# Layer 0's feed-forward in a two-layer fp32 backbone: both halves of the context's columns as one moving operand of 512, their partial sums added on VectorE

## The chip, the cores and the metric

The kernel runs on one core of one Trainium2 chip. The metric is the device time of one execution in microseconds (us), lower is better. All sums below are made on one profiled execution of the kernel before.

## What is computed

A two-layer backbone over 512 latent tokens and 256 context tokens, width 1024, everything in fp32. Each layer has an attention sub-layer and a channel sub-layer. The change touches the channel sub-layer of layer 0 alone. Cut to what matters (latents and context run through the same weights, each with its own shift, scale and gate):

```python
def conv_ffn(h, w_up, conv_w, conv_b, w_down):
    u = h @ w_up                                   # 1024 -> 2 * 2816
    u = depthwise_conv_width_3(u, conv_w) + conv_b # along the tokens
    g, v = jnp.split(u, 2, axis=-1)
    return (jax.nn.silu(g) * v) @ w_down

hx = modulate(rmsnorm(x_lat, g_ffn[l]), sh2x, sc2x)
x_lat = x_lat + g2x * conv_ffn(hx, w_up[l], conv_w[l], conv_b[l], w_down[l])
if not last:                                       # layer 0 only
    hc = modulate(rmsnorm(x_ctx, g_ffn[l]), sh2c, sc2c)
    x_ctx = x_ctx + g2c * conv_ffn(hc, w_up[l], conv_w[l], conv_b[l], w_down[l])
```

The last layer has no context in its feed-forward, so a context product of the feed-forward exists in layer 0 only.

## The kernel before

**Products in three parts.** Activations lie with their features on the partitions and the 768 tokens along the free dimension: latents in columns 0 to 511, context in 512 to 767. Each fp32 factor is split into a high half (rounded to the fp32r type) and a low half (the rest): weights `w_hi` and `w_lo`, activations `h_hi` and `h_lo` (input of the up-projection), `a_hi` and `a_lo` (input of the down-projection). For each block k of 128 input features the function `three` issues three matmuls into one PSUM bank: w_hi with the high half, w_hi with the low half, w_lo with the high half (lines 1289, 1290, 1291). Each has its own weight load.

**Units.** A unit is 128 output features. It has two PSUM banks: bank `bank_of(c)` for the 512 latent columns, the next for the 256 context columns (`groups` is `[(0, 512), (512, 768)]` in layer 0). Four units take turns in the eight banks (`RING` = 4), and four slots in `w_hi` and `w_lo` do so too. The up-projection has 44 units in layer 0 (22 pairs of a g unit and a v unit), each over 8 blocks k. They come in three parts of 8, 8 and 6 pairs (`PARTS`); behind each part come 8 down units over as many k as the part had pairs, so 22 k for each of the 8 output tiles.

**TensorE's order in layer 0's feed-forward.** `first_units` does the first three up units together, k by k, latents first, since each k of `h_hi`, `h_lo` comes just then from VectorE. Then `feature_unit` does one unit after the other: all k of the latents, then all k of the context. `down_start` does the first two down units of a part in two batches: all but the last two k, then these, behind a wait for the last pair's `a_lo` (`a_lo_done`). The last four down units of the last part are `tail_units`: the latents of all four, then the context of all four, with the sums of squares (L1255) and the spreading of the norm's factor (L1235) between. Then layer 1's projection begins, `first_tiles`, again k by k as VectorE delivers `h_lo`.

**What follows a unit.** For an up unit ScalarE (L2112) writes the convolution's middle tap and bias from PSUM to `conv_g` or `conv_v`, one instruction for the latents and one for the context. Then it rounds the next weights of this slot (`unit_hi`, L1737, from `w_raw`), GpSimd subtracts them for `w_lo` (L1164), and that frees the `w_raw` buffer for a DMA from the queue on SyncE. VectorE (L2666) adds the two outer taps from PSUM, latents and context each, with one wait on itself between the two taps. For a pair it then multiplies (L2675), ScalarE rounds (`a_hi`, L2121), VectorE subtracts (`a_lo`, L2678). Between pairs VectorE also reduces tiles of the modulation's weights (`ada_tile`, L2158). For a down unit VectorE adds the gated result into `x_sb` (`update`, L2621, in the tail `update_part`, L2333), latents and context each one instruction.

**The tail on VectorE.** `tail` mixes, in a fixed order: updates of the four last tiles (L2333), sums of squares (L2261, fed by ScalarE's squares), the reciprocal for the norm (L2255), one weight split (L2208), and for each k the next layer's normed input (`ht`, L2288, and `h_lo`, L2296). The context's updates of tiles 2 and 3 stand between the latents' k, the context's norm factor behind the last of them:

```python
for k in range(1, KT):
    part_scaled(j, 0, k)
    part_lo(j, 0, k - 1)
    if k in (1, 3):
        update_part(1, 2 + k // 2)
    if k in (2, 4):
        add_part(j, 1, 1 + k // 2)
part_lo(j, 0, KT - 1)
part_scales(j, 1)
```

## Time and profile before

| | us |
|---|---|
| median of 3 runs | 1715.58 |
| lowest and highest of them | 1715.50, 1716.35 |
| span of the profiled execution, its own time | 1715.9 |
| TensorE busy in it | 1643.9 |
| VectorE busy in it | 1101.3 |
| ScalarE busy in it | 773.7 |
| GpSimd busy in it | 634.2 |

The profiled execution has no time of its own beside the span from its first to its last instruction. Layer 0's feed-forward lies between 456.7 us (first matmul of its up-projection) and 1010.5 us (first matmul of layer 1) of that span. PE is TensorE's matmul, PEld its weight load, DVE VectorE, ACT ScalarE, POOL GpSimd. Matmuls overlap: the duration in a row is longer than the distance from one start to the next, and the distance is what a matmul costs in a row of them.

### The profile page before, as it was taken

The numbers are of one execution on the slowest core, as the hardware profiler recorded it, in microseconds if no ns is written. First come the engines' busy times: TensorE is split into PE (matmuls) and PEld (weight loads), VectorE is DVE, ScalarE is ACT, GpSimd is POOL, SyncE is SP. The second block draws the span as 40 slices with busy tenths as digits, with TensorE's granted clock in tenths as the row PEclk, the third lists the DMA queues.
The fourth block names the chain that finished last, engine by engine and source line by source line (L and its number), as shares of the span: only waits on it lengthen the run. The fifth ranks groups of instructions, "written<-read, shape, count | busy, mean of one in ns | idle before, by whom it ended". The sixth has DMA issues, their size and how long they took to land.

```text
span 1715.9 us, 25956 instructions
## 1 busy us (share of the span) xinstructions
PE 1643.9 (96%) x9530; PEld 1393.6 (81%) x9530; DVE 1101.3 (64%) x1728; ACT 773.7 (45%) x1281; POOL 634.2 (37%) x328
## 2 busy tenths in 40 slices
PE   5899999989999999999999999999989999999998
PEld 3778887768898888888888877788767888888887
DVE  7887678878965575676245774777665763353256
ACT  6546666553443312332133344676564543343343
POOL 0356562220132243333332307664322244444442
PEclk9899999999999999999999999999999999999999
DMA  9430000024223243444434422101112133223332
GB/s 394 176 109 26 26 26 26 26 98 185 80 97 106 98 135 100 133 125 132 136 111 134 147 98 87 38 14 38 38 34 103 62 112 99 97 98 98 95 93 95
DMA packets 44509, 168.24 MB, mean 98 GB/s; under 512 B 4736, under 2 KB 4736, under 8 KB 42496
## 3 DMA queue, kind: packets, MB, share of 16 engines
q1 hardware_dynamic: 41760, 158.08, 27.7%
q10 hardware_dynamic: 2656, 8.91, 1.4%
q8 instruction: 60, 0.98, 0.2%
q14 instruction: 33, 0.27, 0.1%
HBM read 161.73 MB, written 5.24 MB: 97 GB/s over the span
## 4 chain that ended last, share of the span: by engine, by line
PE 70%; DVE 6%; issue 3%; ACT 2%; POOL 1%; DMA 1%; DVEq 0%; ACTq 0%; POOLq 0%
PE ps L1289 21%; PE ps L1290 21%; PE ps L1291 21%; PE ps L1420 3%; PE ps L1434 2%; DVE sqsum L2261 1%; PE ps L1453 1%; POOL w_lo L1164 1%; DVE ht L2288 1%; PE ps L1454 1%; DVE junk_mid L2191 1%; DMA w_raw<-w_d 1%; DVE h_lo L2296 1%; ACT p_sb L1966 0%; ACT w_hi L1737 0%
## 5 line engine op out<-in xcount | busy, mean ns | idle before, releaser
L1164 POOL TENSOR_TENSOR w_lo<-w_raw,w_hi 128x1024 fp32r<-128x1024 f32 x175 | 441.3, 2524 | 915.4 <-ACT w_hi L1737 882.7
L1289 PE MATMUL ps<-h_hi,w_hi 128*128 128x512 f32 (+1 forms) x1592 | 567.7, 357 | 10.8 <-DVE h_lo L2296 6.5
L1290 PE MATMUL ps<-h_lo,w_hi 128*128 128x512 f32 (+1 forms) x1592 | 556.1, 349 | 0.0
L1291 PE MATMUL ps<-h_hi,w_lo 128*128 128x512 f32 (+1 forms) x1592 | 555.4, 349 | 0.0
L1289 PEld LDWEIGHTS ps<-h_hi,w_hi 128*128 128x128 f32 x1592 | 302.5, 190 | 59.3 <-issue 21.0
L1291 PEld LDWEIGHTS ps<-h_hi,w_lo 128*128 128x128 f32 x1592 | 302.3, 190 | 39.7
L1290 PEld LDWEIGHTS ps<-h_lo,w_hi 128*128 128x128 f32 x1592 | 302.9, 190 | 35.3
L1737 ACT ACTIVATE w_hi<-w_raw 128x1024 fp32r<-128x1024 f32 x188 | 198.4, 1056 | 227.9 <-PE ps L1291 209.8
L1289 PE MATMUL ps<-a_hi,w_hi 128*128 128x512 f32 (+1 forms) x552 | 191.6, 347 | 1.2 <-DVE a_lo L2678 1.2
L1290 PE MATMUL ps<-a_lo,w_hi 128*128 128x512 f32 (+1 forms) x552 | 191.3, 347 | 0.0
L1291 PE MATMUL ps<-a_hi,w_lo 128*128 128x512 f32 (+1 forms) x552 | 191.0, 346 | 0.0
L2666 DVE SCALAR_TENSOR_TENSOR conv_v<-ps,sm,conv_v 128x511 f32<-128x511 f32 (+1 forms) x132 | 83.2, 658 | 140.3 <-ACT conv_v L2112 134.0
L2463 DVE TENSOR_REDUCE nb<-ps 128x1 f32<-128x768 f32 (+1 forms) x160 | 128.8, 843 | 11.2 <-PE ps L1420 10.9
L1211 POOL TENSOR_TENSOR p_sb<-p_sb,ri 128x768 f32<-128x768 f32 (+1 forms) x80 | 105.2, 1335 | 77.5 <-DVE ri L2470 77.5
L2488 DVE TENSOR_TENSOR pt_lo<-ps,pt_hi 128x512 fp32r<-128x512 f32 (+1 forms) x160 | 105.9, 673 | 40.0 <-ACT pt_hi L1976 39.4
L2666 DVE SCALAR_TENSOR_TENSOR conv_g<-ps,sm,conv_g 128x511 f32<-128x511 f32 (+1 forms) x132 | 83.1, 658 | 69.1 <-ACT conv_g L2112 57.5
L1966 ACT ACTIVATE p_sb<-ps,nb 128x768 f32<-128x768 f32 (+1 forms) x120 | 97.1, 813 | 62.0 <-DVE nb L2463 51.6
L2621 DVE SCALAR_TENSOR_TENSOR x_sb<-ps,mod,x_sb 128x512 f32<-128x512 f32 x72 | 45.3, 657 | 121.9 <-PE ps L1291 121.6
L2112 ACT ACTIVATE conv_v<-ps,sm 128x512 f32<-128x512 f32 x66 | 44.3, 705 | 166.8 <-PE ps L1291 166.8
L1976 ACT ACTIVATE pt_hi<-ps 128x512 fp32r<-128x512 f32 (+1 forms) x160 | 91.5, 586 | 59.6 <-PE ps L1434 56.0
L2158 DVE CUSTOM_DVE_ANT_0 ada_junk<-ada_b,c_bc 128x1024 bf16<-128x1024 f32 x80 | 117.0, 1463 | 2.0 <-DMA ada_b<-ada_d 0.7
L1289 PEld LDWEIGHTS ps<-a_hi,w_hi 128*128 128x128 f32 x552 | 104.5, 189 | 14.7 <-DVE a_lo L2678 1.6
(189 smaller groups left out, 2410.7 us busy)
## 6 DMA issues: line engine op xcount, KB each, us to landing
w_raw<-w_d SPq DMA_DIRECT2D x188, 512.0 KB, 3.5
ada_b<-ada_d SPq DMA_DIRECT2D x56, 512.0 KB, 4.3
ada_first<-first_d SPq DMA_DIRECT2D x8, 1024.0 KB, 20.3
ada_lead<-ada_d SPq DMA_DIRECT2D x14, 512.0 KB, 3.9
ada_mid<-ada_d SPq DMA_DIRECT2D x10, 512.0 KB, 7.8
x_sb<-x_d SPq DMA_DIRECT2D x2, 1536.0 KB, 8.8
x_sb<-x_d ACTq DMA_DIRECT2D x1, 3072.0 KB, 11.6
x_spill_d<-x_sb ACTq DMA_DIRECT2D x1, 2048.0 KB, 7.5
```

The costliest lines, as they stand in the source:

```text
L1164: nc.gpsimd.tensor_tensor(w_lo[:, c % RING, :], w_raw[:, c % RAW, :], w_hi[:, c % RING, :].bitcast(f32), ALU.subtract).then_inc(w_lo_done, 1)
L1211: nc.gpsimd.tensor_tensor(buf, buf, ri[:, r:r + 1].broadcast_to([P, k]), ALU.mult).then_inc(scaled_done, 1)
L1289: nc.tensor.matmul(out, lh, rh, start=first, stop=False)
L1290: nc.tensor.matmul(out, lh, rl_, start=False, stop=False)
L1291: return nc.tensor.matmul(out, ll, rh, start=False, stop=last)
L1737: A(w_hi[:, c % RING, :], w_raw[:, c % RAW, :], ACT.Copy).then_inc(w_hi_done, 1)
L1966: A(dst, src, ACT.Exp, bias=nb[:, sid % 8:sid % 8 + 1], accum_out=total).then_inc(exp_done, 1)
L1976: A(pt_hi[tid % TURNS][:, 0:n], ps[:, 4 + tid % TURNS, 0:n], ACT.Copy).then_inc(pt_hi_done, 1)
L2158: ins = V.tensor_tensor_reduce(junk[:, :], buf[:, :], silu_c[:, s, :], 1.0, 0.0, ALU.mult, ALU.add, dst(s))
L2463: V.tensor_reduce(nb[:, sid % 8:sid % 8 + 1], src, AX.X, ALU.max, negate=True).then_inc(bias_done, 1)
L2488: V.tensor_tensor(lo[:, 0:n], ps[:, 4 + tid % TURNS, 0:n], hi[:, 0:n].bitcast(f32), ALU.subtract) \
L2666: ins = V.scalar_tensor_tensor(dst, src, sm[:, bass.ds(8 * i + w, 1)], dst, ALU.mult, ALU.add)
```

## The change

In layer 0's feed-forward the context's product of a block k is made by two matmuls in place of three. `h_hi` and `h_lo` become the two planes of one tensor `h_both`, `a_hi` and `a_lo` those of `a_both` (the same addresses as before for `h`, and for `a`). One matmul takes w_hi with a moving operand of 2 x 256 columns, the high half's context columns and the low half's, and writes 512 columns of the context's bank. The second takes w_lo with the high half and adds to the first 256 of them. The bank then holds two partial sums of 256 columns, and VectorE adds them: for an up unit by a reduction over two strided elements into `ctx_sum` in SBUF, after which it also makes the context's middle tap and bias itself (ScalarE does the latents' only), and the outer taps of the context read `ctx_sum`; for a down unit by one more gated add into `x_sb`. In the tail the second add waits for the first. The latents, layer 1, the attention's products and the output projection stay as they are.

```diff
+            def beside(c, lhs, both, k, first, last):
+
+                lh, ll = lhs
+                out = ps[:, bank_of(c) + 1, :]
+                both = both[:, :, k, SEQ:TOK]
+
+                def low():
+                    return nc.tensor.matmul(out[:, 0:CTX], ll, both[:, 0, :], start=False, stop=False)
+
+                if not first:
+                    low()
+                mm = nc.tensor.matmul(out[:, 0:2 * CTX].rearrange("p (a t) -> p a t", a=2), lh, both, start=first, stop=last)
+                return low() if first else mm
...
                 for g, (t0, t1) in enumerate(groups):
                     for k in range(kn):
                         col = slice(k * P, (k + 1) * P)
-                        mm = three(ps[:, bank_of(c) + g, 0:t1 - t0], (w_hi[:, c % RING, col], w_lo[:, c % RING, col]),
-                                   (mh[:, k, t0:t1], ml[:, k, t0:t1]), k == 0, k == kn - 1)
+                        lhs = w_hi[:, c % RING, col], w_lo[:, c % RING, col]
+                        if g == 1:
+                            mm = beside(c, lhs, moving, k, k == 0, k == kn - 1)
+                        else:
+                            mm = three(ps[:, bank_of(c), 0:t1 - t0], lhs,
+                                       (moving[:, 0, k, t0:t1], moving[:, 1, k, t0:t1]), k == 0, k == kn - 1)
...
-                                for g, (t0, t1) in enumerate(groups):
-                                    ins = A(buf[:, t0:t1], tile_out(l, c, g), ACT.Identity,
-                                            bias=sm[:, bass.ds(8 * i + (wcol + 3), 1)],
-                                            scale=sm[:, bass.ds(8 * i + (wcol + 1), 1)])
-                                ins.then_inc(conv_started, 1)
+                                A(buf[:, 0:SEQ], tile_out(l, c, 0), ACT.Identity,
+                                  bias=sm[:, bass.ds(8 * i + (wcol + 3), 1)],
+                                  scale=sm[:, bass.ds(8 * i + (wcol + 1), 1)]).then_inc(conv_started, 1)
                                 unit_hi(c + RING, i)
...
+                    sums = [ps[:, bank_of(c + n) + i, 0:t1 - t0]]
+                    if j % 2 == 0 and in_halves(l, g):
+                        sums = half_sums(c + n)
+                    for m, src in enumerate(sums):
+                        ins = V.scalar_tensor_tensor(xs, src, mod[:, g, l * N_ADA + gate + d:l * N_ADA + gate + d + 1],
+                                                     xs, ALU.mult, ALU.add)
+                        if m < len(sums) - 1:
+                            step(ins)
+                    ins.then_inc(bank_read if i else tail_read, 1)
...
+                    if halves:
+                        step.mark(add(1, half_sums(c)[0]))
+                    ins = add(0, ps[:, bank_of(c), 0:SEQ])
+                    if halves:
+                        step.wait()
+                        ins = add(1, half_sums(c)[1])
+                    elif len(groups) > 1:
+                        ins = add(1, ps[:, bank_of(c) + 1, 0:CTX])
                     ins.then_inc(bank_read, 1)
...
+                                if l == 0:
+                                    wait_tile(dve, c, i)
+                                    two = ps[:, bank_of(c) + 1, 0:2 * CTX].rearrange("p (a t) -> p t a", a=2)
+                                    step(V.tensor_reduce(ctx_sum[:, gv, :], two, AX.X, ALU.add))
+                                    step.mark(V.tensor_scalar(buf[:, SEQ:TOK], ctx_sum[:, gv, :],
+                                                              sm[:, bass.ds(8 * i + (wcol + 1), 1)],
+                                                              sm[:, bass.ds(8 * i + (wcol + 3), 1)], ALU.mult, ALU.add))
                                 dve.wait_ge(conv_started, 4 * i + (2 * (pair0 + half) + gv + 1))
-
+                                if l == 0:
+                                    step.wait()
                                 for tap in range(2):
                                     w = wcol + 2 * tap
                                     for g, (t0, t1) in enumerate(groups):
                                         dst = buf[:, t0 + 1:t1] if tap == 0 else buf[:, t0:t1 - 1]
                                         n_ = t1 - t0
-                                        whole = tile_out(l, c, g)
+                                        whole = ctx_sum[:, gv, :] if g == 1 else tile_out(l, c, g)
```

`first_units`, `down_start` and `tail_units` call `beside` for the context in the same way. `step(ins)` is an instruction and a wait of VectorE for its end; `step.mark` counts it, `step.wait` waits later.

## Rows read from the trace of the kernel before

**Rows 1.** The page, busy time of the span and the chain that ended last.
```profile
PE 1643.9 (96%) x9530; PEld 1393.6 (81%) x9530; DVE 1101.3 (64%) x1728; ACT 773.7 (45%) x1281; POOL 634.2 (37%) x328
...
PE 70%; DVE 6%; issue 3%; ACT 2%; POOL 1%; DMA 1%; DVEq 0%; ACTq 0%; POOLq 0%
```
**Rows 2.** Windows: stretch, its length, busy of each engine (instructions), granted clock.
```profile
456.70:999.80 543.10, 543.04 (x3105) 479.63 (x3106) 334.43 (x495) 170.44 (x228) 173.32 (x64) 1.00 0.36 118
```
**Rows 3.** Groups by line and form, PE, window 456.7:999.8: count, busy, mean ns.
```profile
L1289 PE MATMUL ps<-h_hi,w_hi 128*128 128x256 f32 x352 | 99.4, 282 | 0.0
...
L1291 PE MATMUL ps<-a_hi,w_lo 128*128 128x256 f32 x152 | 43.0, 283 | 0.0
```
**Rows 4.** Timeline, PE, two runs of one form: start, duration (us).
```profile
480.07 0.28 PE L1290 MATMUL ps<-h_lo,w_hi 128*128 128x256 f32 x1
...
482.71 0.28 PE L1291 MATMUL ps<-h_hi,w_lo 128*128 128x256 f32 x1
482.83 0.40 PE L1289 MATMUL ps<-h_hi,w_hi 128*128 128x512 f32 x1
...
484.21 0.39 PE L1289 MATMUL ps<-h_hi,w_hi 128*128 128x512 f32 x1
...
488.07 0.39 PE L1291 MATMUL ps<-h_hi,w_lo 128*128 128x512 f32 x1
```
**Rows 5.** Timeline, PE, layer 0's first tiles: three of 512, three of 256, again.
```profile
53.56 0.40 PE L1289 MATMUL ps<-h_hi,w_hi 128*128 128x512 f32 x1
...
54.61 0.40 PE L1289 MATMUL ps<-h_hi,w_hi 128*128 128x512 f32 x1
```
**Rows 6.** Groups by line and form, DVE and, last, ACT, whole span.
```profile
L2463 DVE TENSOR_REDUCE nb<-ps 128x1 f32<-128x768 f32 x128 | 116.5, 950 | 10.4 <-PE ps L1420 10.1
...
L2463 DVE TENSOR_REDUCE nb<-ps 128x1 f32<-128x256 f32 x32 | 12.3, 416 | 0.8 <-PE ps L1420 0.8
...
L2621 DVE SCALAR_TENSOR_TENSOR x_sb<-ps,mod,x_sb 128x256 f32<-128x256 f32 x24 | 11.4, 475 | 0.0
...
L2479 DVE TENSOR_SCALAR rl<-ri,nlam,first_sum 128x1 f32<-128x1 f32 x40 | 10.9, 273 | 1.4
...
L2112 ACT ACTIVATE conv_v<-ps,sm 128x512 f32<-128x512 f32 x44 | 34.3, 779 | 166.8 <-PE ps L1291 166.8
```
**Rows 7.** Timeline, DVE and ACT, one pair of part 1 and the first taps.
```profile
726.44 2.42 DVE L2666 SCALAR_TENSOR_TENSOR conv_v<-ps,sm,conv_v 128x511 f32<-128x511 f32 x4 [4.46 <-ACT conv_v L2112]
...
731.70 0.96 DVE L2678 TENSOR_TENSOR a_lo<-conv_g,a_hi 128x768 f32 x1 [1.16 <-ACT a_hi L2121]
...
725.06 1.24 ACT L2112 ACTIVATE conv_v<-ps,sm 128x512 f32<-128x512 f32 x2 [6.08 <-PE ps L1291]
...
485.32 1.14 DVE L2666 SCALAR_TENSOR_TENSOR conv_g<-ps,sm,conv_g 128x511 f32<-128x511 f32 x2 [0.16 <-DVE conv_g L2666]
```
**Rows 8.** Timeline, the end of part 2's up-projection: DVE, then PE.
```profile
965.28 0.96 DVE L2678 TENSOR_TENSOR a_lo<-conv_g,a_hi 128x768 f32 x1 [1.16 <-ACT a_hi L2121]
...
966.64 0.40 PE L1289 MATMUL ps<-a_hi,w_hi 128*128 128x512 f32 x1
```
**Rows 9.** Timeline, the tail and layer 1's start: DVE, then PE.
```profile
995.83 0.75 DVE L2333 SCALAR_TENSOR_TENSOR x_sb<-ps,mod,x_sb 128x512 f32<-128x512 f32 x1 [2.73 <-PE ps L1291]
...
1003.61 0.18 DVE L2255 RECIPROCAL n_r<-n_sd 128x4 f32<-128x4 f32 x1 [1.06 <-ACT n_sd L1747]
...
1006.62 1.23 DVE L2208 TENSOR_TENSOR w_lo<-w_raw,w_hi 128x1024 fp32r<-128x1024 f32 x1 [0.34 <-ACT w_hi L1737]
...
1012.71 0.43 DVE L2261 TENSOR_TENSOR sqsum<-sqsum,sqt 128x256 f32<-128x256 f32 x1 [0.83 <-ACT sqt L1871]
...
1014.37 0.48 DVE L2333 SCALAR_TENSOR_TENSOR x_sb<-ps,mod,x_sb 128x256 f32<-128x256 f32 x1
...
1014.51 0.50 PE L1289 MATMUL ps<-h_hi,w_hi 128*128 128x512 f32 x1 [0.93 <-DVE h_lo L2296]
...
1021.73 0.71 PE L1235 MATMUL ps<-sm,n_r 128*128 128x128 f32 x4 [1.71 <-DVE n_r L2255]
```

More of the change, by code:

```diff
@@ L707, in backbone @@
     sqsum = place("sqsum", [P, TOK], f32, R_QKV + 48 * KB)
-    h_hi = place("h_hi", [P, KT, TOK], f32r, R_H)
-    h_lo = place("h_lo", [P, KT, TOK], f32r, R_H + 24 * KB)
+    h_both = place("h_both", [P, 2, KT, TOK], f32r, R_H)
+    h_hi, h_lo = h_both[:, 0, :, :], h_both[:, 1, :, :]
     y_sb = place("y_sb", [P, 2, KT, SEQ // 2], f32, R_H)
@@ L713, in backbone @@
     ol = place("ol", [P, KT, TOK], f32r, R_QKV + 24 * KB)
-    a_hi = place("a_hi", [P, 8, TOK], f32r, R_QKV)
-    a_lo = place("a_lo", [P, 8, TOK], f32r, R_QKV + 24 * KB)
+    a_both = place("a_both", [P, 2, 8, TOK], f32r, R_QKV)
+    a_hi, a_lo = a_both[:, 0, :, :], a_both[:, 1, :, :]
     o_sb = place("o_sb", [P, KT, TOK], f32, R_O)
@@ L718, in backbone @@
     conv_v = place("conv_v", [P, TOK], f32, R_O + 3 * KB)
+    ctx_sum = place("ctx_sum", [P, 2, CTX], f32, R_O + 22 * KB)
     sqt = place("sqt", [P, 2, TOK], f32, R_O)
@@ L1016, in tile_out, with in_halves, half_sums @@
             return ps[:, bank_of(c) + g, 0:t1 - t0]
+        def in_halves(l, g):
+            return l == 0 and g == 1
+        def half_sums(c):
+            return ps[:, bank_of(c) + 1, 0:CTX], ps[:, bank_of(c) + 1, CTX:2 * CTX]
         stat_order = [("norm", 0, 0)]
@@ L1275, in tail_units @@
                                 lhs = (w_hi[:, w[0], w[1]], w_lo[:, w[0], w[1]])
-                                rhs = (moving[0][:, k, t0:t1], moving[1][:, k, t0:t1])
+                                rhs = (moving[:, 0, k, t0:t1], moving[:, 1, k, t0:t1])
                             else:
                                 lhs, rhs = half_weights(l, KT - TAIL + n, k, True), half_output(k, True, t0, t1)
-                            mm = three(ps[:, bank_of(c + n) + i, 0:t1 - t0], lhs, rhs, k == 0, k == kn - 1)
+                            if moving and in_halves(l, g):
+                                mm = beside(c + n, lhs, moving, k, k == 0, k == kn - 1)
+                            else:
+                                mm = three(ps[:, bank_of(c + n) + i, 0:t1 - t0], lhs, rhs, k == 0, k == kn - 1)
                         mm.then_inc(unit_done if i else tail_done, 1)
@@ L1597, in feature_unit @@
                     pe.wait_ge(bank_read, 4 * i + (evac_index(c) - 3))
-                mh, ml = moving
                 for g, (t0, t1) in enumerate(groups):
@@ L1618, in first_units @@
                             w = ((c + j) % RING, slice(k * P, (k + 1) * P))
-                            mm = three(part_out(norm, c + j, i),
-                                       (w_hi[:, w[0], w[1]], w_lo[:, w[0], w[1]]),
-                                       (h_hi[:, k, t0:t1], h_lo[:, k, t0:t1]), k == 0, k == KT - 1)
+                            lhs = w_hi[:, w[0], w[1]], w_lo[:, w[0], w[1]]
+                            if g == 1:
+                                mm = beside(c + j, lhs, h_both, k, k == 0, k == KT - 1)
+                            else:
+                                mm = three(part_out(norm, c + j, i), lhs, (h_hi[:, k, t0:t1], h_lo[:, k, t0:t1]),
+                                           k == 0, k == KT - 1)
                             if k == KT - 1 and i == 1:
@@ L1679, in down_start @@
                                 w = ((c + j) % RING, slice(k * P, (k + 1) * P))
-                                mm = three(ps[:, bank_of(c + j) + g, 0:t1 - t0],
-                                           (w_hi[:, w[0], w[1]], w_lo[:, w[0], w[1]]),
-                                           (a_hi[:, k, t0:t1], a_lo[:, k, t0:t1]), k == 0, k == n - 1)
+                                lhs = w_hi[:, w[0], w[1]], w_lo[:, w[0], w[1]]
+                                if g == 1:
+                                    mm = beside(c + j, lhs, a_both, k, k == 0, k == n - 1)
+                                else:
+                                    mm = three(ps[:, bank_of(c + j), 0:t1 - t0], lhs,
+                                               (a_hi[:, k, t0:t1], a_lo[:, k, t0:t1]), k == 0, k == n - 1)
                         if ks[0] > 0:
@@ L2614, in _, with update, add @@
                     ada_late(2)
-                def update(c, gate, x_col):
+                def update(c, gate, x_col, halves=False):
                     wait_tile(dve, c)
-                    for g, (t0, t1) in enumerate(groups):
-                        xs = x_sb[:, x_col, t0:t1]
-                        ins = V.scalar_tensor_tensor(xs, ps[:, bank_of(c) + g, 0:t1 - t0],
-                                                     mod[:, g, l * N_ADA + gate + x_col:l * N_ADA + gate + x_col + 1],
-                                                     xs, ALU.mult, ALU.add)
+                    def add(g, src):
+                        xs = x_sb[:, x_col, groups[g][0]:groups[g][1]]
+                        factor = mod[:, g, l * N_ADA + gate + x_col:l * N_ADA + gate + x_col + 1]
+                        return V.scalar_tensor_tensor(xs, src, factor, xs, ALU.mult, ALU.add)
+                    if halves:
[6 more added lines that the diff above has]
+                        ins = add(1, ps[:, bank_of(c) + 1, 0:CTX])
                     ins.then_inc(bank_read, 1)
@@ L2697, in _ @@
                     if l == 0:
-                        per += [4, 5, 1][part]
+                        per += [4, 5, 1][part] + 2 * 2 * 2
                     split = l == DEPTH - 1 and part == 0
@@ L2707, in _ @@
                         c = down_unit(l, part) + d
-                        update(c, 5 * KT, d)
+                        update(c, 5 * KT, d, in_halves(l, len(groups) - 1))
                         if l == 0 and d < ADA_IN_DOWN[part]:
```

12 lines of the change are left out of this document (5 added, 7 removed).

## The prediction

> **What bounds the kernel now.** I read the page first. TensorE is busy for 96% of the span and carries 70% of the chain that ended last, VectorE 6% of it [rows 1]. So the question for every part of the change is whether it lies on TensorE's path. The stretch that the change touches, by its window, is tighter still: from 456.7 to 999.8 us TensorE is busy for 543.04 of 543.10 us at the full granted clock (1.00, that is 2.4 GHz), VectorE for 334, ScalarE for 170 [rows 2]. The reader is to see that there is no wait there to be removed: a gain can only come from fewer nanoseconds in TensorE's own row of matmuls, and VectorE has 209 us of room. The tail behind it is another matter: there TensorE waits for VectorE twice, 0.93 and 1.71 us [rows 9].
>
> Next the timeline, for what one matmul costs in a row of them. 22 distances of the form 256 take 2.64 us (480.07 to 482.71), 120.0 ns each; 17 of the form 512 take 3.86 us (484.21 to 488.07), 227.1 ns each [rows 4]. The second 256 columns cost 107.1 ns, so the first 256 cost the same plus 12.9 ns. That 12.9 ns is the fixed share of a matmul with its weight load, and it is what the change can save.
>
> **The change part by part: TensorE.** Three matmuls of 256 columns (360.0 ns) become one of 512 and one of 256 (347.1 ns). The columns streamed are the same 768, the weight loads go from three to two: 12.9 ns less for each k. The forms' counts say how often: 352 such k in the up-projections and 152 in the down-projections of this stretch, 504 in all [rows 3]; 24 more lie in the tail.
>
> The row of matmuls now changes its form at almost every step. What such changes cost is to be seen in layer 0's first tiles, where three of 512 and three of 256 take turns: one round takes 1.05 us (53.56 to 54.61) against 3 x 347.1 = 1.041 us, 9 ns more for one change each way [rows 5]. With runs of one, the bounds are nothing and the whole 9 ns for each k. I take 3 ns, a third, since the excess could be spread over the three matmuls that follow the change as well as sit on the first. That leaves 10 ns for each k: 504 x 0.010 = 5.0 us, with ends of 504 x 0.004 = 2.0 and 504 x 0.0129 = 6.5 us.
>
> The moving operand now lies in two pieces of 256 columns. No row shows such an operand. The bounds: nothing, or, if the second piece begins like a matmul of its own, 2 x 120.0 - 227.1 = 13 ns for each k, which would take the whole saving. I see no reason for a gain from it, and take nothing, as an address step is nearer to the middle of a matmul than to a new one.
>
> The Trainium skill ("TensorE: Matmul & The Clock Gate", Back-to-back issue gap) gives N / 2.4 + 2.5 ns from one matmul to the next at full clock. By it the three matmuls cost 327.5 ns and the two 325.0, and the change would be worth 504 x 0.0025 = 1.3 us. The trace disagrees: its fixed share is 12.9 ns [rows 4].
>
> **VectorE and ScalarE in the up units.** ScalarE loses its context instruction: of 1.24 us for both [rows 7] 0.78 stay [rows 6]. VectorE gets a reduction over 512 PSUM elements; rows for 256 and 768 elements take 416 and 950 ns, so 0.68 us between them. It is strided, which no row shows; its end could lie up to twice as high. Then a wait for itself, 0.16 us as between the taps [rows 7], then the context's middle tap over 256 elements of SBUF. For that there is only a form of one element, 0.27 us, and a two-tensor form of 256, 0.48 [rows 6]; I take 0.40. Then 0.16 again. The taps could start 0.68 + 0.16 + 0.40 + 0.16 = 1.40 us behind the unit's end. Before, they started 726.44 - 725.06 = 1.38 us behind it, as they waited for ScalarE [rows 7]. So nothing is late for a unit whose end VectorE waits for. The Trainium skill ("VectorE: DVE Perf Modes", The TRN2 errata) has 58 + 256/2 cycles, 0.19 us, for the tap if it runs in the doubled mode. No row here shows that mode; it would make the start earlier by 0.2 us, with the same sum.
>
> VectorE's work grows by about 2 x 1.4 = 2.8 us for a pair. In a pair of part 1 it stands idle 4.46 + 1.16 = 5.6 us of the 16.7 that TensorE takes [rows 7], so it still fits. Behind VectorE's added wait stand only its own taps, and behind these the PSUM bank and ScalarE. The bank is wanted four units later: the first taps end at 486.5 us [rows 7] and TensorE wants that bank when the unit started at 482.83 [rows 4] has ended, 24 x (0.227 + 0.120) = 8.3 us on, at 491.2. A delay of 1.4 us is covered by 4.7. `w_hi`, `w_lo` and the DMA behind them come a little sooner, since ScalarE rounds after a shorter instruction; TensorE waits for none of them here, so this is worth nothing.
>
> The tightest place is the end of part 2's up-projection. The last `a_lo` ends at 966.24 us and TensorE wants it at 966.64, 0.40 us later [rows 8]. TensorE comes 8 x 0.010 = 0.08 us sooner, the pair's chain starts 0.02 later: 0.3 us of cover stay. If the added instructions took 1 us more than I sum, that would cost 0.7 us, once.
>
> **VectorE in the down units.** One more instruction of 0.48 us [rows 6] for each of 20 units outside the tail, with the wait placed behind the latents' add, so hardly a stall. TensorE's unit takes 6 to 8 us beside it. Four of them lie before the tail, about 1.8 us that VectorE brings with it; it is waiting 2.73 us for TensorE before the third tail update [rows 9], which takes them up.
>
> **The tail.** Here VectorE is the path, and the two adds of a tile depend on each other: 0.48 + 0.16 = 0.64 us more for each of four tiles. Tile 0's lies under the wait of 1.06 us for the norm's root. Tile 1's meets 0.34 us of idle before the weight split [rows 9] and a context that ends 0.07 us sooner: 0.23 late. Tile 2's makes that 0.87, of which the 0.83 us of idle before its squares (ScalarE, itself behind a weight's DMA) take all but 0.04. Tile 3's, at 1014.37, meets no idle. So the norm factor, for which TensorE waits 1.71 us at 1021.73 [rows 9], comes 0.68 us later, and layer 1 with it. The 24 k saved in the tail end in those waits and are worth nothing. Bounds: 0 if the waits absorb all, 2.6 if all four are exposed.
>
> **Sum.** 1715.9 - 5.0 + 0.7 = 1711.6 us on the profiled execution's scale. It lies 0.3 us above the median of the runs, so the forecast for the median is 1711.3, call it 1711.2. A difference of 0.2%, 3.4 us, is about what a measurement of this kernel can tell from none; the edges are 1712.1 and 1719.0.
>
> **The rivals.**
>
> A. The forecast: 9 to 13 ns saved for each k, a small loss in the tail. 1709 to 1712. For it: 256 more columns cost 107.1 ns, which is 2.4 GHz to half a nanosecond, so the rest of either form is no streaming, and TensorE never waits in the stretch. Chance 0.62.
>
> B. Too little is saved to be seen. If the full 9 ns of a change each way falls on each k, 4 ns stay: 2.0 - 0.7 = 1.3 us, 1714.3. The same outcome follows if the fixed share belongs to something that two matmuls of unlike form do not share. By the Trainium skill's gap ("TensorE: Matmul & The Clock Gate", Back-to-back issue gap) it would be 1.3 - 0.7, 1715.0, the same case. For it: the round of six really is longer [rows 5]. Against it: in that round the change touches one matmul in three. Chance 0.25, all of it within 0.2%.
>
> C. The split operand costs a fixed share of its own: 347.1 + 13 + 3 ns against 360.0 for each k, 1.5 us lost, and 0.7 in the tail: 1717.8. It decides against the change from 9 ns on, and visibly from 17 ns on. Chance 0.08, half of it above 1719.0.
>
> D. VectorE becomes what TensorE waits for in the loop of pairs: a wait for `bank_read` or `w_lo` takes the place of free running. Its price: from 5.6 us of added work for a pair on, each further microsecond is paid in each of 22 pairs; at 6.6 us it is 22 - 4.3 = 18 us, 1733. That needs the strided reduction at some 2.6 us in place of 0.68. Against it: VectorE has 209 us of room [rows 2]. Chance 0.05, slower.
>
> **The numbers.** Faster 0.62, same 0.25 + 0.04 = 0.29, slower 0.09. The range goes from 1709.0 (12.9 ns saved in full, the tail almost free) to 1716.8 (beyond B, into the milder half of C).
>
> **What would show it.** After the change, the distances in TensorE's row within the context's k should sum to about 350 ns for one 512 and one 256; 347 means that changes of form are free, 356 is rival B, 363 rival C. VectorE's busy time in the stretch should rise by some 60 us, ScalarE's fall by 20, and TensorE's idle time should stay under 1 us. In the tail the wait for `n_r` should grow by 0.7 us. I am wrong if a wait for `bank_read`, `w_lo` or `a_lo` appears inside the stretch, or if the pair of matmuls leaves 345 to 353 ns.

## The result, and the profile after

The changed kernel takes 1746.95 us (median of 4 runs, 1742.62 to 1749.37) against 1715.96 of the kernel before (4 runs beside it, 1715.50 to 1720.17). The ratio is 1.017, with a 95% interval of 1.015 to 1.019: 31 us slower, where I forecast 4 us faster and put the upper end of my range at 1716.8. The profiled execution has a span of 1745.3 us, against 1715.9.

First the page of the changed kernel, the busy times and the chain that ended last.

```profile
PE 1645.8 (94%) x9002; PEld 1367.9 (78%) x9002; DVE 1224.2 (70%) x1840; ACT 755.3 (43%) x1237; POOL 625.0 (36%) x328
...
PE 52%; DVE 17%; issue 9%; ACT 3%; DVEq 1%; POOL 1%; DMA 0%; ACTq 0%; SPq 0%; POOLq 0%
```

TensorE has its 528 fewer matmuls (9530 in [rows 1], 9002 now), but VectorE's busy time grew by 123 us and its share of the chain from 6% to 17%. Next, what TensorE waited for from the first up unit to the tail's end: us in total, times, longest.

```profile
PE ps L1315 <- DVE a_both L2734: 24.4, 3, 11.2
PE ps L1315 <- DVE h_both L2329: 2.3, 2, 1.8
PE ps L1244 <- DVE n_r L2288: 1.7, 1, 1.7
PE ps L1315 <- DVE conv_g L2722: 1.4, 2, 0.8
```

L2734 is the subtraction that was `a_lo`. It makes TensorE wait three times, once at the end of each part: 24.4 us in a stretch that had no wait at all [rows 2]. L2722 are the outer taps, which free a PSUM bank: 1.4 us. Both are waits that the prediction named as signs of its being wrong. `n_r` is the wait of [rows 9], unchanged at 1.7.

Then the windows of the changed kernel: stretch, length, busy us of PE, PEld, DVE, ACT and POOL (instructions), granted clock, DMA share, GB/s.

```profile
457.00:998.00 541.00, 515.23 (x2460) 431.47 (x2459) 430.07 (x570) 142.16 (x172) 154.25 (x61) 0.97 0.34 111
...
613.00:619.00 6.00, 5.52 (x14) 4.42 (x15) 4.67 (x12) 1.06 (x1) 0.14 (x1) 0.52 0.27 87
```

VectorE is busy for 430 us where it was for 334 [rows 2], and TensorE for 515 of 541. Behind the first wait the granted clock is 0.52. The timeline of TensorE there:

```profile
603.35 0.40 PE L1309 MATMUL ps<-a_both,w_hi 128*128 128x512 f32 x1
613.48 0.80 PE L1315 MATMUL ps<-a_both,w_hi 128*128 128x512 f32 x1 [9.73 <-DVE a_both L2734]
614.07 0.63 PE L1316 MATMUL ps<-a_both,w_hi 128*128 128x512 f32 x1
614.50 0.63 PE L1317 MATMUL ps<-a_both,w_lo 128*128 128x512 f32 x1
...
618.77 0.41 PE L1315 MATMUL ps<-a_both,w_hi 128*128 128x512 f32 x1
619.01 0.40 PE L1316 MATMUL ps<-a_both,w_hi 128*128 128x512 f32 x1
```

After standing for 9.7 us TensorE comes back at 1.2 GHz: 0.43 us from one matmul of 512 to the next, until 618.77, then 0.24 us. Those 5.29 us hold 11 matmuls of 512 and 2 of 256, which at the distances of [rows 4] are 2.74 us; so the wait costs some 2.6 us more than its own length. The second wait (11.2 us, up to 826.00) is followed by 4.4 us at half clock, worth 2.1. After the third (3.5 us, up to 993.12) TensorE runs 1.0 us at full clock and then 3.3 us at 0.51, worth 1.6. That is 6.3 us in all. From the first up matmul to the tail's first sums of squares the trace has 574.2 us, before 545.4: 28.9 us more. The parts give 24.4 + 1.4 + 6.3, less the 4.2 that TensorE saved (measured in e2_tensor_only below): 27.9. The last 1.0 us is not accounted for.

### The profile page after: what moved, and what is told of

Read it like the earlier page. It is cut to its first block, busy times and chain, and to the rows that moved or that the text cites. A ratio compares the mean times of both kernels' runs of the same rounds, so it can differ in the third digit from the quotient of the medians.

```text
span 1745.3 us, 25175 instructions
## 1 busy us (share of the span) xinstructions
PE 1645.8 (94%) x9002; PEld 1367.9 (78%) x9002; DVE 1224.2 (70%) x1840; ACT 755.3 (43%) x1237; POOL 625.0 (36%) x328
## 4 chain that ended last, share of the span: by engine, by line
PE 52%; DVE 17%; issue 9%; ACT 3%; DVEq 1%; POOL 1%; DMA 0%; ACTq 0%; SPq 0%; POOLq 0%
PE ps L1315 14%; PE ps L1317 13%; PE ps L1316 13%; PE ps L1446 3%; PE ps L1309 3%; DVE conv_g L2722 2%; PE ps L1460 2%; DVE conv_v L2722 2%; DVE ctx_sum L2708 1%; PE ps L1305 1%; DVE ada_junk L2191 1%; DVE conv_g L2731 1%; DVE conv_g L2709 1%; ACT a_both L2154 1%; DVE mod L2748 1%
## 5 line engine op out<-in xcount | busy, mean ns | idle before, releaser
L1315 PE MATMUL ps<-h_both,w_hi 128*128 128x512 f32 (+1 forms) x1240 | 468.0, 377 | 12.7 <-DVE h_both L2329 7.9
L1317 PE MATMUL ps<-h_both,w_lo 128*128 128x512 f32 (+1 forms) x1240 | 456.0, 368 | 0.0
L1316 PE MATMUL ps<-h_both,w_hi 128*128 128x512 f32 (+1 forms) x1240 | 455.7, 367 | 0.0
L1315 PEld LDWEIGHTS ps<-h_both,w_hi 128*128 128x128 f32 x1240 | 234.7, 189 | 59.9 <-issue 23.0
L1317 PEld LDWEIGHTS ps<-h_both,w_lo 128*128 128x128 f32 x1240 | 234.6, 189 | 39.6
L1316 PEld LDWEIGHTS ps<-h_both,w_hi 128*128 128x128 f32 x1240 | 235.2, 190 | 35.5
L1315 PE MATMUL ps<-a_both,w_hi 128*128 128x512 f32 (+1 forms) x376 | 143.9, 383 | 26.5 <-DVE a_both L2734 25.7
L2191 DVE CUSTOM_DVE_ANT_0 ada_junk<-ada_b,c_bc 128x1024 bf16<-128x1024 f32 x80 | 145.5, 1819 | 1.3
L1317 PE MATMUL ps<-a_both,w_lo 128*128 128x512 f32 (+1 forms) x376 | 143.0, 380 | 0.0
L1316 PE MATMUL ps<-a_both,w_hi 128*128 128x512 f32 (+1 forms) x376 | 142.9, 380 | 0.0
L1309 PE MATMUL ps<-h_both,w_hi 128*128 128x512 f32 x352 | 127.5, 397 | 0.0
L2662 DVE SCALAR_TENSOR_TENSOR x_sb<-ps,mod,x_sb 128x512 f32<-128x512 f32 (+1 forms) x92 | 53.1, 616 | 101.6 <-PE ps L1317 67.1
L2722 DVE SCALAR_TENSOR_TENSOR conv_v<-ps,sm,conv_v 128x511 f32<-128x511 f32 x88 | 66.0, 750 | 58.7 <-ACT conv_v L2146 49.3
L1315 PEld LDWEIGHTS ps<-a_both,w_hi 128*128 128x128 f32 x376 | 72.0, 191 | 40.3 <-DVE a_both L2734 27.0
```

Source lines behind the costliest of these rows:

```text
L1309: mm = nc.tensor.matmul(out[:, 0:2 * CTX].rearrange("p (a t) -> p a t", a=2), lh, both, start=first, stop=last)
L1315: nc.tensor.matmul(out, lh, rh, start=first, stop=False)
L1316: nc.tensor.matmul(out, lh, rl_, start=False, stop=False)
L1317: return nc.tensor.matmul(out, ll, rh, start=False, stop=last)
L2191: ins = V.tensor_tensor_reduce(junk[:, :], buf[:, :], silu_c[:, s, :], 1.0, 0.0, ALU.mult, ALU.add, dst(s))
L2722: ins = V.scalar_tensor_tensor(dst, src, sm[:, bass.ds(8 * i + w, 1)], dst, ALU.mult, ALU.add)
```

## Why VectorE is late: the same instruction at two prices

VectorE's groups by form in the stretch of the feed-forward of the changed kernel: busy us, mean ns of one, then idle time before.

```profile
L2191 DVE CUSTOM_DVE_ANT_0 ada_junk<-ada_b,c_bc 128x1024 bf16<-128x1024 f32 x80 | 145.5, 1819 | 1.3
L2722 DVE SCALAR_TENSOR_TENSOR conv_g<-ctx_sum,sm,conv_g 128x255 f32<-128x255 f32 x44 | 38.6, 878 | 0.0
L2722 DVE SCALAR_TENSOR_TENSOR conv_v<-ps,sm,conv_v 128x511 f32<-128x511 f32 x44 | 33.0, 750 | 6.4
L2708 DVE TENSOR_REDUCE ctx_sum<-ps 128x256 f32<-128x512 f32 x44 | 30.2, 685 | 20.3 <-PE ps L1309 16.6 <-DVE mod L2748 1.7 <-DVE mod L2750 1.2
L2722 DVE SCALAR_TENSOR_TENSOR conv_v<-ctx_sum,sm,conv_v 128x255 f32<-128x255 f32 x44 | 27.1, 615 | 0.0
...
L2709 DVE TENSOR_SCALAR conv_g<-ctx_sum,sm 128x256 f32<-128x256 f32 x22 | 21.0, 955 | 5.1 <-DVE ctx_sum L2708 5.1
...
L2748 DVE COPY mod<-ada_sum 128x2 f32 x16 | 18.7, 1166 | 2.3
...
L2709 DVE TENSOR_SCALAR conv_v<-ctx_sum,sm 128x256 f32<-128x256 f32 x22 | 14.1, 641 | 4.2 <-DVE ctx_sum L2708 4.2
```

The reduction costs what I gave it, 0.68. But the context's outer tap, 255 elements, takes 878 ns in its mean for a g unit, longer than the latents' of 511 elements at 750, and 615 for a v unit; the middle tap takes 955 and 641 ns. Single instructions show why. VectorE, then GpSimd, at the end of part 0:

```profile
600.18 0.68 DVE L2708 TENSOR_REDUCE ctx_sum<-ps 128x256 f32<-128x512 f32 x1
601.06 1.61 DVE L2709 TENSOR_SCALAR conv_g<-ctx_sum,sm 128x256 f32<-128x256 f32 x1 [0.19 <-DVE ctx_sum L2708]
602.82 0.75 DVE L2722 SCALAR_TENSOR_TENSOR conv_g<-ps,sm,conv_g 128x511 f32<-128x511 f32 x1 [0.15 <-DVE conv_g L2709]
603.49 1.69 DVE L2722 SCALAR_TENSOR_TENSOR conv_g<-ctx_sum,sm,conv_g 128x255 f32<-128x255 f32 x1
605.33 0.75 DVE L2722 SCALAR_TENSOR_TENSOR conv_g<-ps,sm,conv_g 128x511 f32<-128x511 f32 x1 [0.15 <-DVE conv_g L2722]
606.00 0.48 DVE L2722 SCALAR_TENSOR_TENSOR conv_g<-ctx_sum,sm,conv_g 128x255 f32<-128x255 f32 x1
606.39 0.69 DVE L2708 TENSOR_REDUCE ctx_sum<-ps 128x256 f32<-128x512 f32 x1
607.27 0.41 DVE L2709 TENSOR_SCALAR conv_v<-ctx_sum,sm 128x256 f32<-128x256 f32 x1 [0.19 <-DVE ctx_sum L2708]
...
612.47 0.96 DVE L2734 TENSOR_TENSOR a_both<-conv_g,a_both 128x768 f32 x1 [1.16 <-ACT a_both L2154]
```
```profile
599.83 5.06 POOL L1173 TENSOR_TENSOR w_lo<-w_raw,w_hi 128x1024 fp32r<-128x1024 f32 x2 [13.46 <-ACT w_hi L1772]
```

GpSimd does two splits of a weight from 599.83 to 604.89, so one ends near 602.3 and the next near 604.9. The middle tap takes 0.41 us at 607.27, when GpSimd is idle, and 1.61 us at 601.06: it ends at 602.67, which is about the first split's end and its own 0.41. The outer tap takes 0.48 at 606.00 and 1.69 at 603.49: it ends at 605.18, some 0.3 us behind the second split's end (the trace is rough for GpSimd). The taps between them that read PSUM take 0.75 us, split or no split. These rows suggest that an instruction of VectorE that reads two operands from SBUF, or a TENSOR_SCALAR or COPY from SBUF to SBUF, stands still until GpSimd's running split is over, and that one with an operand in PSUM does not; e5 and e6 below test it. The change moved four outer context taps for a pair from the second kind to the first and added two middle taps of the first.

The Trainium skill ("SBUF — State Buffer", SBUF: two separate sides) states the rule: an instruction of VectorE in a two-port mode, or with two SBUF inputs where GpSimd's instruction reads SBUF too, and one of GpSimd exclude each other for the whole instruction, and the loser stands. The trace agrees, with 0.41 against 1.61 us for the middle tap and 0.48 against 1.69 for the outer one.

The sign was in the trace before. Four groups of VectorE by form, kernel before, same stretch:

```profile
L2158 DVE CUSTOM_DVE_ANT_0 ada_junk<-ada_b,c_bc 128x1024 bf16<-128x1024 f32 x80 | 117.0, 1463 | 2.0 <-DMA ada_b<-ada_d 0.7
L2675 DVE TENSOR_TENSOR conv_g<-conv_g,conv_v 128x768 f32<-128x768 f32 x22 | 34.8, 1582 | 0.8
...
L2678 DVE TENSOR_TENSOR a_lo<-conv_g,a_hi 128x768 f32 x22 | 21.1, 959 | 25.1 <-ACT a_hi L2121 25.1
...
L2692 DVE COPY mod<-ada_sum 128x2 f32 x16 | 10.8, 674 | 2.2
```

The product L2675 and the subtraction L2678 are two instructions of one form, 1582 and 959 ns: the product fell under GpSimd's split, the subtraction never did. I read only the second price.

The busy times now nearly add up. The times without a split are 413 ns for the middle tap, 475 for the outer tap, 1224 for an ada tile, 959 for the product and 178 for a copy (ada tile and copy from e5_small_split below). Against them the changed kernel stands 47.6 us in its 80 ada tiles, 23.9 in its outer taps, 16.9 in its middle taps, 15.8 in 16 copies and 3.9 in three others, 108 us; the kernel before stood 19.1 + 13.7 + 7.9 = 41 us in ada tiles, products and copies. That is 67 us more of standing, beside 58 us of real new work (44 x 0.685 + 44 x 0.413 + 20 x 0.477) and 2 us in the tail: 127, against the page's difference of 123, in which what overlaps counts once.

What it means for the pairs: in part 0 the subtraction L2734 starts at 510.15 and six pairs later at 612.47, 17.05 us for a pair, 15.6 and 18.5 in turn. TensorE takes 16 x (3 x 0.227 + 0.353) = 16.55. So VectorE does not catch up with the three units that it gets at once at the start of part 0. Part 1 has no such start, but three ada tiles for each pair in place of two, and from 694.73 to 824.98 a pair takes 18.6 us: the backlog of some 14 us grows there from the pace alone, and this part ends in the longest wait. In part 2 a pair takes 17.06 us (906.82 to 992.11), and the wait is 3.5 us.

## The experiments

**TensorE alone, VectorE alone.** Is TensorE's part worth what I summed, and is the loss all VectorE's? e2_tensor_only keeps the new matmuls and gives ScalarE and VectorE their old work (the reduction and the second adds go, and the second partial sum stays unread); e3_vector_only keeps the new ScalarE and VectorE work on the three old matmuls and adds the one partial sum to itself.

```diff
 e2_tensor_only
-        A(buf[:, 0:SEQ], tile_out(l, c, 0), ...)
+        for g, (t0, t1) in enumerate(groups): ins = A(buf[:, t0:t1], tile_out(l, c, g), ...)
...
-        whole = ctx_sum[:, gv, :] if g == 1 else tile_out(l, c, g)
+        whole = tile_out(l, c, g)
 e3_vector_only
+        return three(out[:, 0:CTX], lhs, (both[:, 0, :], both[:, 1, :]), first, last)
...
-        two = ps[:, bank_of(c) + 1, 0:2 * CTX].rearrange("p (a t) -> p t a", a=2)
+        two = ps[:, bank_of(c) + 1, 0:CTX].rearrange("p (t a) -> p t a", a=1).broadcast_to([P, CTX, 2])
```

> TensorE's part of the change alone; VectorE and ScalarE work as before and read only the first partial sum (the second, w_hi with the low half, is left out of the context's result). Theory VectorE (the loss comes from VectorE's added work alone): no wait for a_lo or a bank in layer 0's feed-forward, the clock stays at 1.00 there, and 504 pairs of matmuls at 354 ns in place of 360 give about 3 us: 1713 us. Theory TensorE (the new matmuls themselves cost): waits or longer distances stay, over 1725 us.

> The work of VectorE and ScalarE of the changed kernel alone: TensorE issues the three matmuls as before, and VectorE adds the first 256 columns to themselves in the place of the two partial sums (the context's result is about doubled before the gate). Theory VectorE: the waits at the ends of the three parts are there in full, about 11, 11 and 3.5 us, a little less since TensorE is slower: 1745 us. Theory TensorE: about 1717 us.

e2_tensor_only: 1714.91 us, ratio 0.9983 (0.9972 to 0.9993). Its stretch up to the tail takes 541.2 us against 545.4, 4.2 less, with no wait for `a_both` or a bank. e3_vector_only: 1744.79 us, ratio 1.016 (1.014 to 1.019), and TensorE's waits in it:

```profile
PE ps L1309 <- DVE a_both L2728: 21.1, 3, 10.4
...
PE ps L1309 <- DVE conv_g L2716: 0.6, 1, 0.6
```

So the loss is VectorE's side alone, and TensorE's side is a gain of some 4 us. Its timeline, e2_tensor_only, context matmuls:

```profile
490.62 0.40 PE L1309 MATMUL ps<-h_both,w_hi 128*128 128x512 f32 x1
490.85 0.28 PE L1305 MATMUL ps<-h_both,w_lo 128*128 128x256 f32 x1
490.97 0.40 PE L1309 MATMUL ps<-h_both,w_hi 128*128 128x512 f32 x1
...
492.74 0.40 PE L1309 MATMUL ps<-h_both,w_hi 128*128 128x512 f32 x1
```

Six k take 2.12 us, 353 ns for each. Three matmuls of 256 took 360.0 and two of unchanged distance would take 347.1: inside a unit the saving is 7 ns for each k, and a change of form each way costs about 6. Over the whole context of a unit, whose first k has its two matmuls in the other order, the same trace has 2.81 us for 8 k (490.16 to 492.97), 351 ns each; 504 x 8.7 ns are 4.4 us, which is the stretch's 4.2.

**The operand in two pieces.** e4_one_piece is e2_tensor_only with the moving operand of 512 taken as one piece (the latents' high half, so the context's product is another one).

```diff
+    whole, both = both[:, 0, k, 0:SEQ], both[:, :, k, SEQ:TOK]
...
-    mm = nc.tensor.matmul(out[:, 0:2 * CTX].rearrange("p (a t) -> p a t", a=2), lh, both, start=first, stop=last)
+    mm = nc.tensor.matmul(out[:, 0:2 * CTX], lh, whole, start=first, stop=last)
```

> As the run with TensorE's part alone, but the matmul of 512 reads the latents' high half, one contiguous piece, in place of the context's two pieces (the context's result is not computed). If the split operand costs, the distance behind the 512 falls from 236 to 227 to 233 ns; if the change of form costs, it stays at 233 to 236 ns.

1710.80 us in a single run, span 1709.0, stretch 541.2 us like e2_tensor_only's, and the same distances. The split operand costs nothing; rival C is out. The 4 us by which this single time lies under e2's median are not in the stretch, and I read nothing from them.

**GpSimd's split made small.** If VectorE stands for GpSimd, an eighth of the split (the rest of `w_lo` is left stale) must bring VectorE's instructions back to their prices, with all of the change kept.

```diff
-    nc.gpsimd.tensor_tensor(w_lo[:, c % RING, :], w_raw[:, c % RAW, :], w_hi[:, c % RING, :]..., ALU.subtract)
+    w = slice(0, UNIT // 8 if up_unit(0, 0) + RING <= c < unit0(1) else UNIT)
+    nc.gpsimd.tensor_tensor(w_lo[:, c % RING, w], w_raw[:, c % RAW, w], w_hi[:, c % RING, w]..., ALU.subtract)
```

> The changed kernel, but in layer 0's feed-forward GpSimd writes only the first 128 of 1024 columns of w_lo (most of the weights' low halves are stale). Theory port (VectorE's added instructions on two SBUF operands, or in the form that reads SBUF doubly, stand still while GpSimd works): their means fall from 878, 615, 955 and 641 ns to about 0.47, 0.47, 0.41 and 0.41 us, the copies to mod to 0.25, a pair takes VectorE under 15 us, TensorE waits nowhere, about 1712 us. Theory sum (the added instructions and their waits are too long in themselves): a pair still takes 16 to 18 us and the time stays over 1735.

1715.06 us, ratio 0.9984 (0.9973 to 0.9994), and no wait for `a_both`. VectorE's groups by form in it:

```profile
L2192 DVE CUSTOM_DVE_ANT_0 ada_junk<-ada_b,c_bc 128x1024 bf16<-128x1024 f32 x80 | 97.9, 1224 | 1.7 <-DMA ada_b<-ada_d 0.3
...
L2723 DVE SCALAR_TENSOR_TENSOR conv_g<-ctx_sum,sm,conv_g 128x255 f32<-128x255 f32 x44 | 21.4, 486 | 0.0
L2710 DVE TENSOR_SCALAR conv_g<-ctx_sum,sm 128x256 f32<-128x256 f32 x22 | 9.6, 436 | 5.1 <-DVE ctx_sum L2709 5.1
L2710 DVE TENSOR_SCALAR conv_v<-ctx_sum,sm 128x256 f32<-128x256 f32 x22 | 9.1, 413 | 4.2 <-DVE ctx_sum L2709 4.2
```

955 became 436 ns, 878 became 486, 1819 became 1224. Where VectorE runs through its backlog in part 0 a pair takes 13.2 and 14.5 us in turn, 13.9 in the mean. By my sum it was 16.7 - 5.6 + 2.8 = 13.9, and that agreement is luck. The pair that I summed was one of part 1 [rows 7], with three ada tiles and no copies, where part 0 has two tiles, and copies in every other pair; it held 0.7 us of a standing product; and my 5.6 us counted the 1.16 us for ScalarE's rounding as room, which e5's pairs contain. The added work itself was summed about right. A pair of part 1 without copies takes 16.7 - 4.46 - 0.68 = 11.6 us before (without its wait for the unit and the standing) and 16.63 - 1.91 = 14.7 in e5, 3.1 us more where I had 2.8. With the copies the next pair takes 16.15, so 15.4 in the mean. To TensorE's 16.55 that leaves 2.7 us of room in part 0 and 1.1 in part 1, and the changed kernel takes 3.2 us more than e5 in both, 17.05 and 18.6.

**Which form stands.** e6_taps_from_psum keeps every instruction and wait of the change, but both the middle tap and the outer taps of the context read the first partial sum in PSUM in place of `ctx_sum` (so the second partial sum is left out). e10_middle_from_psum does it for the middle tap alone, e11_outer_from_psum for the outer taps alone.

```diff
 e6, e10
-    step.mark(V.tensor_scalar(buf[:, SEQ:TOK], ctx_sum[:, gv, :], ...))
+    step.mark(V.tensor_scalar(buf[:, SEQ:TOK], half_sums(c)[0], ...))
 e6, e11
-    whole = ctx_sum[:, gv, :] if g == 1 else tile_out(l, c, g)
+    whole = half_sums(c)[0] if g == 1 else tile_out(l, c, g)
```

> The changed kernel with every instruction and wait of it, but the context's middle tap and outer taps on VectorE read the first partial sum in PSUM in place of the sum in SBUF (the second partial sum is left out of the up-projection's context). Theory port: an instruction with one SBUF operand at most does not stand still behind GpSimd, so the taps of 255 stay at 0.48 us and the middle tap at 0.4 to 0.5; a pair takes VectorE under 15.5 us and TensorE no longer waits for a_lo: 1712 to 1716 us. Theory sum: 1740 us or more.

> The changed kernel, only the context's middle tap on VectorE reads the first partial sum in PSUM; the outer taps still read the sum in SBUF (part of the context's convolution is left wrong). It takes the doubled form away and leaves the two-operand form. In the changed kernel's trace the middle tap stood still for (955 + 641 - 2 x 413) x 22 ns = 17 us, the outer taps for (878 + 615 - 2 x 475) x 44 ns = 24 us. If both forms hold VectorE, about half of the 28 us of loss stays: 1725 to 1735 us. If only the doubled form does, 1714.

> The counterpart: the outer taps of the context read PSUM, the middle tap reads the sum in SBUF in its doubled form. If both forms hold VectorE, 1718 to 1730 us, a little less than the run before, since its share was 24 of 41 us. If only the two-operand form does, 1714; if only the doubled form does, 1745.

A single run each: 1713.96, 1738.79 and 1724.78 us. TensorE's wait for `a_both` is 24.4 us in the changed kernel, and in e6, e10 and e11 in this order:

```profile
PE ps L1315 <- DVE a_both L2734: 1.5, 2, 0.9
```
```profile
PE ps L1315 <- DVE a_both L2734: 18.8, 3, 8.9
```
```profile
PE ps L1315 <- DVE a_both L2734: 8.0, 2, 5.1
```

Both forms hold VectorE, the outer taps' two SBUF operands more (22 us of time come back without them, 8 without the middle tap's, 33 without both). The time that one form loses is partly taken over by the next that meets the split. In e11 the middle tap stands longer than in the changed kernel (955 ns there):

```profile
L2709 DVE TENSOR_SCALAR conv_g<-ctx_sum,sm 128x256 f32<-128x256 f32 x22 | 25.0, 1134 | 5.1 <-DVE ctx_sum L2708 5.1
```

So it counts what meets the split, and the price is the split's remainder, not a slowness of the instruction. With e6 a pair of part 0 takes 16.1 us on VectorE, under TensorE's 16.55, though its middle tap is dearer by itself (544 ns from PSUM against 413 from SBUF). In part 1 it takes 17.4, since the ada tiles still stand (1722 ns in their mean). VectorE falls behind there too, but no wait for `a_both` is longer than 0.9 us; that the first down units, which start without the last pair, cover the rest is argued, not shown. The same instructions and waits end 33 us sooner.

**A version that keeps the gain.** e7_add_in_psum makes the same sums as the change: ScalarE copies the second partial sum to SBUF, VectorE adds it in place in PSUM, and middle tap (ScalarE again) and outer taps read PSUM as in the kernel before.

```diff
+    A(ctx_sum[:, gv, :], half_sums(c)[1], ACT.Copy).then_inc(ctx_copied, 1)
...
+    act.wait_ge(ctx_added, ...)
+    A(act_scrap[:, :], sm[:, 0:1], ACT.Copy)
...
-    step(V.tensor_reduce(ctx_sum[:, gv, :], two, AX.X, ALU.add))
-    step.mark(V.tensor_scalar(buf[:, SEQ:TOK], ctx_sum[:, gv, :], ..., ALU.mult, ALU.add))
+    dve.wait_ge(ctx_copied, ...)
+    lo = half_sums(c)[0]
+    V.tensor_tensor(lo, lo, ctx_sum[:, gv, :], ALU.add).then_inc(ctx_added, 1)
```

e8_one_form adds that the context's matmuls of a unit go form by form, all k with w_hi, then all k with w_lo; e9_tail_in_three adds that the four tail units keep three matmuls for the context and one update.

```diff
 e8_one_form
+    for narrow in (False, True):
+        for c in units:
+            for k in ks:
+                mm = ... w_lo with 256 columns if narrow else w_hi with 512 ...
 e9_tail_in_three, in tail_units
-    beside([c + n], range(kn), moving, kn - 1)
+    mm = three(ps[:, bank_of(c + n) + i, 0:t1 - t0], lhs, rhs, k == 0, k == kn - 1)
```

> The two partial sums of an up unit added otherwise: ScalarE copies the second to SBUF (about 0.4 us), VectorE adds it to the first in PSUM (one SBUF operand, about 0.42 us), and taps and ScalarE's middle tap are those of before the change. Down units and tail as in the change. Theory port: VectorE's pair takes 12 to 13 us, no wait for a_lo but perhaps some 0.5 us at the end of part 2, the full gain of the 504 pairs (504 x 0.006 = 3 us) less 0.7 in the tail: ratio 0.9985. Theory sum: also under 16 us, so the same; it tells only whether the change can be made to pay.

> The run with the add in PSUM, and in TensorE's row matmuls of one form together: for a unit's context all of 512 first, then all of 256 (in the first three up units for each k the three of 512, then the three of 256). If the change of form costs, the 8 + 8 matmuls take 8 x 347 + 20 ns in place of 8 x 353: about 0.03 us less for each of 44 up units and 0.02 for each down unit, 1.5 to 2 us in all. If the distance of 353 belongs to the two forms themselves, nothing.

> As the last, but the tail's context is made in three matmuls of 256 as before the change, with one add on VectorE. By the working of the prediction the second adds put 0.7 us on VectorE's path there, and the saved time of TensorE is worth nothing: 0.7 us less than the last run, and the wait for n_r goes back to 1.71 us behind the same start. If the adds lay under other waits, no difference.

| | us | ratio to before (95%) | stretch up to the tail, us |
|---|---|---|---|
| kernel before | 1716.74 | | 545.35 |
| e7_add_in_psum | 1713.58 | 0.9975 (0.9965 to 0.9986) | 541.32 |
| e8_one_form | 1711.80 | 0.9977 (0.9964 to 0.9990) | 538.82 |
| e9_tail_in_three | 1709.97 | 0.9953 (0.9936 to 0.9969) | 538.82 |

The ratio is taken between runs made side by side, so it doesn't follow the medians to the last tenth. The window of the feed-forward in e7_add_in_psum:

```profile
457.00:998.00 541.00, 539.21 (x2603) 452.66 (x2603) 366.03 (x563) 190.56 (x317) 156.00 (x64) 1.00 0.37 119
```

VectorE is busy for 366 us, not 430; TensorE has its full clock and no wait. The stretches of e8 and e9 are 6.53 us shorter than before's. e9's holds the 504 changed k and no more, 12.96 ns each (e8's has six more, and a wait of 0.17 us): with the forms together the whole fixed share of the prediction comes out. The timeline of e8_one_form, one unit's context:

```profile
488.46 1.98 PE L1312 MATMUL ps<-h_both,w_hi 128*128 128x512 f32 x8
490.27 1.11 PE L1309 MATMUL ps<-h_both,w_lo 128*128 128x256 f32 x8
491.23 0.40 PE L1320 MATMUL ps<-h_both,w_hi 128*128 128x512 f32 x1
```

Eight of 512 take 1.81 us and eight of 256 take 0.96: 226 and 120 ns, the distances of [rows 4]. From the first sums of squares in the tail to the matmul that spreads `n_r` e8 takes 19.76 us and e9 18.69: the second adds in the tail cost 1.07 us, and e9 takes them away. e9 is the fastest, faster than both kernels. The difference of e8 and e9 in median is larger than 1.07 us but within what the runs scatter.

## The prediction, point by point

**The step that failed: "VectorE's work grows by about 2 x 1.4 = 2.8 us for a pair ... so it still fits."** The durations of the added work were right where GpSimd is idle: reduction 0.685 us (0.68), middle tap 0.41 (0.40), its own waits 0.15 to 0.19 (0.16). But I took the outer taps' price from their PSUM form and left it when their operand moved to SBUF, and priced every new instruction as if GpSimd stood idle. The Trainium skill's 0.19 us for the middle tap ("VectorE: DVE Perf Modes", The TRN2 errata) is not what the trace has, 0.41, though the tap is faster from SBUF than from PSUM (0.54 in e6). In the changed order the instructions meet GpSimd's splits: 3.2 us for a pair. I had 2.8 us of room left (16.7 - 13.9); without the 1.16 us that are no room, and with the copies, it was 2.7 in part 0 and 1.1 in part 1. e3 shows that this side alone makes the loss, e5 that GpSimd's split is the cause, e6, e10 and e11 through which operands.

**"VectorE has 209 us of room."** [rows 2] A share of busy time was the wrong measure: VectorE's pair is a chain with waits of its own (1.16 us for ScalarE's rounding, 0.15 to 0.19 behind the reduction and the taps), and between 532 and 548 us of the changed kernel it is busy for 13.6 of 16 us, 2.4 of them standing in two taps, and falls behind all the same.

**Rival D** was the outcome, at 1747 where I gave 1733 and a chance of 0.05. Its price for a pair is about what came, 5.6 us of added time and each further microsecond in full: by the like pairs above, 3.1 + 3.2 = 6.3 us were added in part 1. But this 5.6, too, counted the 1.16 us as room. Its mechanism did not hold: it asked for a reduction of 2.6 us, and that one costs 0.685. It also took TensorE's loss for a wait in the loop of pairs; the ring of four units lets TensorE run ahead, and most of the loss comes due at the three ends of parts, where TensorE waits 9.7, 11.2 and 3.5 us for the last `a_lo`, with some 6 us for the granted clock behind them, which I had nowhere. My cover of 0.40 us at the end of part 2 [rows 8] was read as if the pairs before it ran on time.

**TensorE.** Fixed share 12.9 ns: right, e8 gets all of it. Change of form 3 ns: mis-sized, about 6 measured inside a unit and 4 over a whole one, so 351 to 353 ns for a k where I wrote 350, and 4.2 us in e2's stretch where I summed 5.0. Split operand at nothing: right, by e4. Rival B (356) and rival C (363) are both excluded by the distance. (By rival C's own terms a split operand would have shown from 15 ns on, (1719.0 - 1715.6 - 0.7) / 504 + 10, not from 17.) A sum by the Trainium skill's gap ("TensorE: Matmul & The Clock Gate", Back-to-back issue gap) would have been 1.3 us. At full clock the runs disagree with it, e8's 6.5 us most plainly; at half clock the same section gives N / 1.2, 427 ns for 512 columns, and the trace after the waits agrees (0.43).

**ScalarE and the weights.** "`w_hi`, `w_lo` come a little sooner, worth nothing": the reverse held. When VectorE is late, ScalarE's next activation for a g unit waits for `a_both`, and then the weights of two units are rounded soon after one another. GpSimd then runs two splits in a row (the row of 5.06 us, where before it ran single ones of 2.4), and VectorE's next instructions meet both. In part 2 of the changed kernel the splits are single and VectorE still stands, so the doubling is not needed for the loss; that it feeds the delay is argued from the order of the rows, and no run took it away by itself.

**The tail.** Four second adds at 0.68 us: they cost 1.07 (e8 against e9). Against the kernel before only 0.15 of it shows (19.76 against 19.61 us), since the wait of 0.83 us for ScalarE's squares [rows 9] is absent in the changed kernel and in e9 too. I had it absorb tile 2's add, and it is gone in e9, which has no second add in the tail. Why, no run settles. The wait for `n_r` did not grow by 0.7 (1.69 us); I take it that TensorE's preceding matmuls are paced by VectorE and moved with it. In the down units outside the tail the second adds cost nothing that a run shows.

**What would show it.** VectorE's busy time in the stretch was to rise by 60 us and rose by 96, the excess being time in which it stood behind GpSimd; ScalarE's was to fall by 20 and fell by 28 (170.44 to 142.16, part of it because the stretch holds less work).

## What to carry to other kernels

Before an operand is moved from PSUM to SBUF, or work is added to VectorE beside a GpSimd that computes, look for one form with two mean durations in the trace: the difference can be standing behind GpSimd, which the trace counts as busy time, and every new instruction with two SBUF operands can meet it. Measure room on VectorE as the time of one loop turn with its own waits against TensorE's turn, in the fullest kind of turn, not as a share of busy time. An intermediate sum added in place in PSUM leaves its readers where they were and kept the gain here.

## What the runs showed of the hardware that I had not expected

- VectorE's instructions with two SBUF operands, and TENSOR_SCALAR and COPY from SBUF to SBUF, stand until GpSimd's current split (which reads SBUF) ends: 0.41 becomes 1.61 us, 0.48 becomes 1.69; a pair of copies takes 0.48 us or, under two splits in a row, 4.49. The latents' tap, with one operand in PSUM, takes 0.75 with and without a split.
- The context's middle tap, 256 elements, takes 0.41 us from SBUF and 0.54 from PSUM (e6, e10).
- Matmuls with their own weight load cost 6 ns more for each change from 512 to 256 columns and back (353 against 347 ns); form by form they cost nothing extra.
- A moving operand in two pieces of 256 columns runs like one piece of 512 (e4).
- After the waits of 9.7 and 11.2 us TensorE runs at 1.2 GHz for 5.3 and 4.4 us, so they cost 2.6 and 2.1 us more than their length. After the wait of 3.5 us it comes back at full clock, and the half clock (3.3 us) follows 1.0 us later.
